# Eight edits around TensorE's row of matmuls in a two-layer transformer trunk on one Trainium2 core

## What is computed

```python
def nsa_compress(kv, pos, w1, b1, w2, b2):       # 15 overlapping blocks of 32 tokens
    ...
    hid = jax.nn.gelu(flat @ w1 + b1)
    return hid @ w2 + b2

def nsa_attention(q, k_cmp, v_cmp, k_slc, v_slc, k_win, v_win, gates):
    ...                                           # 8 heads of 64 in 2 groups, queries in blocks of 128
        s_c = jnp.einsum('bgrqd,bgnd->bgrqn', qq, kc)
        p_c = masked_softmax(s_c, cmp_end[None, :] <= tq[:, None])
        o_c = jnp.einsum('bgrqn,bgnd->bgrqd', p_c.astype(vc.dtype), vc)
    ...
    y = gates[..., 0:1] * to_bthd(o_c) + gates[..., 1:2] * to_bthd(o_s) + gates[..., 2:3] * to_bthd(o_w)

def token_mixer(x, w_in, ...):
    hcat = x @ w_in
    ...                                           # y_a: attention, y_b: short convolution, y_c: retention
    proj = jnp.einsum('btcw,cwd->btcd', ys, w_br)
    gates = jax.nn.sigmoid(mgate).reshape(b, t, N_BRANCHES, D_MODEL)
    return jnp.sum(gates * proj, axis=2) @ w_out

def moe_swiglu(x, w_router, w_gate, w_up, w_down):
    logits = (x @ w_router).astype(jnp.float32)
    top_v, top_i = lax.top_k(logits, TOP_K)
    probs = jax.nn.softmax(top_v, axis=-1)
    ...
        out = out + combine[..., e:e + 1] * swiglu(x, w_gate[e], w_up[e], w_down[e])

def reference(x, w_in, ...):
    for l in range(DEPTH):
        m = token_mixer(x, ...)
        x = layer_norm(ALPHA * x + m, ln1_g[l], ln1_b[l])
        if l % 2 == 0:
            f = swiglu(x, ...)
        else:
            f = moe_swiglu(x, ...)
        x = layer_norm(ALPHA * x + f, ln2_g[l], ln2_b[l])
    return x
```

## Time and profile before

| | |
|---|---|
| runs, us | 1846.99, 1847.23, 1847.29 (median 1847.23) |
| profiled execution, own time, us | 1848.0 |
| its span, us | 1846.1 |
| TensorE busy, matmul / weight load | 99% / 86% |
| VectorE, ScalarE, GpSimd busy | 79%, 64%, 3% |
| instructions | 29565 |
| DMA over the span | 511 MB, mean 277 GB/s |
| granted clock, mean | 0.996 |

### The profile page before, as it was taken

How to read it: one execution, slowest core, us unless ns; L and a number is a source line. 1 busy time by engine, 2 the same in 40 slices (tenths; PEclk the granted TensorE clock), 3 DMA queues, 4 the chain that set the end, 5 groups by cost and what they waited for, 6 DMA issues and landing times.

```text
span 1846.1 us, 29565 instructions
## 1 busy us (share of the span) xinstructions
PE 1820.9 (99%) x10905; PEld 1587.3 (86%) x10905; DVE 1457.5 (79%) x1670; ACT 1179.3 (64%) x1441; POOL 56.1 (3%) x37
## 2 busy tenths in 40 slices
PE   9999999999999999999999999999999999999996
PEld 8999998999979999997888888888888888888884
DVE  6675677544566675668999989999999999999998
ACT  6544444443447444446778787787787877877874
POOL 0000000000000000002101001000010010100100
PEclk9999999999999999999999999999999999999998
DMA  9544445555537333455999999999999999999994
GB/s 379 190 162 147 169 165 184 183 196 188 182 137 270 141 138 138 160 206 192 378 375 353 379 362 376 378 337 390 370 354 381 357 376 375 334 395 369 357 381 171
DMA packets 72478, 511.07 MB, mean 277 GB/s; under 512 B 8160, under 2 KB 8544, under 8 KB 11616
## 3 DMA queue, kind: packets, MB, share of 16 engines
q1 hardware_dynamic: 69552, 498.09, 71.4%
q0 software_dynamic: 1584, 5.77, 1.0%
q10 hardware_dynamic: 1280, 6.32, 0.9%
HBM read 508.06 MB, written 2.10 MB: 276 GB/s over the span
## 4 chain that ended last, share of the span: by engine, by line
PE 87%; DVE 6%; ACT 3%; issue 2%; DMA 1%; SPq 0%; DVEq 0%; ACTq 0%
PE PS L398 16%; PE PS L400 16%; PE PS L399 16%; PE PS L371 10%; PE PS L372 10%; PE PS L373 10%; DVE w_lo L1273 2%; DVE w_lo L1270 1%; PE PS L825 1%; DVE merged L1762 1%; ACT w_hi L913 1%; PE PS L557 1%; PE PS L589 1%; PE PS L384 1%; DMA raw<-wstream 1%
## 5 line engine op out<-in xcount | busy, mean ns | idle before, releaser
L1270 DVE TENSOR_TENSOR w_lo<-raw,w_hi 128x1024 fp32r<-128x1024 f32 x471 | 575.3, 1221 | 223.1 <-ACT w_hi L913 221.8
L913 ACT ACTIVATE w_hi<-raw 128x1024 fp32r<-128x1024 f32 x471 | 499.1, 1060 | 274.7 <-PE PS L400 203.6
L1273 DVE TENSOR_TENSOR w_lo<-raw,w_hi 128x1024 fp32r<-128x1024 f32 x471 | 573.4, 1217 | 0.0
L914 ACT ACTIVATE w_hi<-raw 128x1024 fp32r<-128x1024 f32 x471 | 493.5, 1048 | 0.0
L398 PE MATMUL PS<-w_hi,xT_hi 128*128 128x512 f32 x960 | 380.0, 396 | 0.6 <-DVE w_lo L1273 0.2
L371 PE MATMUL PS<-xT_hi,w_hi 128*128 128x256 f32 x1312 | 376.3, 287 | 0.2 <-DVE w_lo L1273 0.2
L400 PE MATMUL PS<-w_hi,xT_lo 128*128 128x512 f32 x960 | 374.5, 390 | 0.0
L399 PE MATMUL PS<-w_lo,xT_hi 128*128 128x512 f32 x960 | 373.8, 389 | 0.0
L372 PE MATMUL PS<-xT_lo,w_hi 128*128 128x256 f32 x1312 | 371.1, 283 | 0.0
L373 PE MATMUL PS<-xT_hi,w_lo 128*128 128x256 f32 x1312 | 371.0, 283 | 0.0
L371 PEld LDWEIGHTS PS<-xT_hi,w_hi 128*128 128x128 f32 x1312 | 251.3, 192 | 9.1 <-issue 6.8
(11 more groups left out here) (261 smaller groups left out, 1567.5 us busy)
## 6 DMA issues: line engine op xcount, KB each, us to landing
raw<-wstream SPq DMA_DIRECT2D x471, 1024.0 KB, 6.8
soft<-ln ACTq DMA_DIRECT2D x4, 1024.0 KB, 5.6
X<-x SPq DMA_DIRECT2D x2, 512.0 KB, 4.1
raw<-wstream SPq DMA_DIRECT2D x4, 256.0 KB, 7.2
x_rows<-X ACTq DMA_DIRECT2D x1, 1024.0 KB, 4.9
out<-X ACTq DMA_DIRECT2D x2, 512.0 KB, 3.7
cst<-consts SPq DMA_DIRECT2D x1, 906.0 KB, 14.5
sm<-small SPq DMA_DIRECT2D x1, 364.5 KB, 15.7
```

The lines of the kernel that those rows point to most:

```text
L913: activate(w_hi[:, at % RING, 0:SUB // 2], src[:, 0:SUB // 2], ACT.Copy).then_inc(half_done, 1)
L914: activate(w_hi[:, at % RING, SUB // 2:SUB], src[:, SUB // 2:SUB], ACT.Copy).then_inc(hi_done, 1)
L1270: v.tensor_tensor(w_lo[:, at % RING, 0:SUB // 2], src[:, 0:SUB // 2], w_hi[:, at % RING, 0:SUB // 2], ALU.subtract)
L1273: v.tensor_tensor(w_lo[:, at % RING, SUB // 2:SUB], src[:, SUB // 2:SUB], w_hi[:, at % RING, SUB // 2:SUB], ALU.subtract).then_inc(lo_done, 1)
```

## The change

- A "cmp" step turns four heads at a time. Probabilities are stored with a pitch of 32 columns per head (`cprobs`), two transposes of 128 x 128 put four heads below one another, and ScalarE alone copies the 256 columns. For this, `Vc` holds for each of four heads V in rows 32n to 32n+14 and zeros else, and the product with it is made per head over 128 rows: four matmuls of 128 columns in place of two of 256. `compressed_kv` makes V for 128 output rows from `hidV`, the hidden values repeated four times at a pitch of 32 (ScalarE writes them so), and VectorE copies four 15-row pieces in place of one. The zeros come from three memsets at the start.
- In the norm after the dense block, tile 0 is taken up in halves like tile 1, on a new semaphore `first_ps`.
- `first_unit` waits for halves of `xT_hi` and `xT_lo` of the second token tile where it needs them.
- The router's fillers go from 7 and 4 to 4 and 3.
- The first subtile is loaded in two transfers; VectorE makes all four quarters of its remainder between the third and the fourth block of `xT_lo`.
- At an item's start, the first two pieces of `add_scattered` stand ahead of the split of subtile 5.
- At the end, statistics of both tiles come ahead of both tiles' scaling, and tile 0's stand between the third and the fourth addition. The store of tile 1 goes in two halves.
- GpSimd's last gather takes 16 rows in place of 128.

```diff
             for t in range(TT):
                 sp.dma_start(X[:, t, :], x[t * P:(t + 1) * P, :]).then_inc(x_in[t], 16)
-            for c in range(4):
-                at = slice(c * SUB // 4, (c + 1) * SUB // 4)
-                sp.dma_start(raw[:, 0, at], wstream[0][:, at]).then_inc(landed[0] if c == 3 else part_in[c], 16)
+            for c in range(2):
+                at = slice(c * SUB // 2, (c + 1) * SUB // 2)
+                sp.dma_start(raw[:, 0, at], wstream[0][:, at]).then_inc(landed[0] if c else part_in, 16)
...
             def first_unit(n, bank, slot, ready=None):
-                pe.wait_ge(xT_hi_rdy, 2 * TT * (n + 1))
+                def high_ready(k):
+                    if k % 4 == 0:
+                        pe.wait_ge(xT_hi_rdy, 2 * TT * n + 3 + k // 4)
+                    if ready:
+                        ready(k)
+
+                def low_ready(k):
+                    if k % 4 == 0:
+                        pe.wait_ge(xT_rdy, 2 * TT * n + 3 + k // 4)
...
                 pe.wait_ge(xT_rdy, 2 * TT * n + 1)
-                o = fm_first(bank, slot, 0, ready)
-                pe.wait_ge(xT_rdy, 2 * TT * (n + 1))
-                fm_first_low(o, slot, 0)
-                return fm_first_low(fm_first(bank, slot, 1), slot, 1)
+                o = fm_first(bank, slot, 0, high_ready)
+                fm_first_low(o, slot, 0, low_ready)
+                return fm_first_low(fm_first(bank, slot, 1, both_ready), slot, 1, both_ready)
...
-                        last = tm_block([o for o in outs if o[1] == t], (s + n) % RING, lhs, ks[n], cols,
-                                        cols == 512 and n == 0, n == 1)
+                        own = [o for o in outs if o[1] == t]
+                        if t == 0 and n == 1 and b is not None:
+                            tm_block(own[:1], (s + n) % RING, lhs, ks[n], cols, False, True).then_inc(first_ps, 1)
+                            own = own[1:]
+                        last = tm_block(own, (s + n) % RING, lhs, ks[n], cols, cols == 512 and n == 0, n == 1)
...
-                        o = PS[0:NC, MB, 64 + g * DH:64 + (g + 1) * DH]
+                        o = PS[:, MB, 64 + g * DH:64 + (g + 1) * DH]
                         for c in range(2):
-                            mm(o, hidT[:, 2 + c, g * NC:(g + 1) * NC], sm[:, l, S_W2V + c * DH:S_W2V + (c + 1) * DH],
+                            mm(o, hidV[:, c, g].rearrange("p a n -> p (a n)"), sm[:, l, S_W2V + c * DH:S_W2V + (c + 1) * DH],
...
                     if kind == "cmp":
-                        for n in range(NH):
-                            last = mm(PS[0:NC, TB + n // 4, (n % 4) * P:(n % 4 + 1) * P], cprob[:, n, :], ident,
-                                      start=True, stop=True)
+                        for par in range(2):
+                            last = nc.tensor.transpose(PS[:, TB, par * P:(par + 1) * P], cprobs[:, 4 * par:4 * par + 4]
+                                                       .rearrange("p i n -> p (i n)"), ident)
...
                     if a == 1:
-                        for par in range(2):
-                            last = mm(o[par], Vc[:, g, :],
-                                      cprobT[0:NC, (4 * par + 2 * g) * P:(4 * par + 2 * g + 2) * P], start=False,
-                                      stop=True, skip_group_check=True)
+                        for e in range(2):
+                            for par in range(2):
+                                last = mm(o[par][:, e * P:(e + 1) * P], Vc[:, 2 * g + e, :],
+                                          cprobT[:, par * P:(par + 1) * P], start=False, stop=True,
+                                          skip_group_check=True)
...
-                stay_busy(7)
+                stay_busy(4)
                 pe.wait_ge(cnt_in, 1)
...
-                stay_busy(4)
+                stay_busy(3)
...
             norm(4)
-            for t in range(TT):
-                act.wait_ge(norm_rdy, 2 * TT * 3 + 2 * t + 2)
-                act.dma_start(out[t * P:(t + 1) * P, :], X[:, t, :]).then_inc(out_dma, 16)
-            act.wait_ge(out_dma, 16 * TT)
+            act.wait_ge(norm_rdy, 2 * TT * 3 + 2)
+            act.dma_start(out[0:P, :], X[:, 0, :]).then_inc(out_dma, 16)
+            act.wait_ge(norm_rdy, 2 * TT * 3 + 3)
+            act.dma_start(out[P:T, 0:512], X[:, 1, 0:512]).then_inc(out_dma, 16)
+            act.wait_ge(norm_rdy, 2 * TT * 3 + 4)
+            act.dma_start(out[P:T, 512:D], X[:, 1, 512:D]).then_inc(out_dma, 16)
+            act.wait_ge(out_dma, 16 * 3)
...
-                nc.gpsimd.indirect_dma_start(xg, None, x_rows, bass.IndirectOffsetOnAxis(ap=rows[:, 0:1], axis=0),
+                few = P if i < NI - 1 else 16
+                nc.gpsimd.indirect_dma_start(xg[0:few], None, x_rows,
+                                             bass.IndirectOffsetOnAxis(ap=rows[0:few, 0:1], axis=0),
...
                 if n < 4:
+                    if n == 2:
+                        dve.wait_ge(half_ps if t else first_ps, 1)
+                        chain.link(add_x(n, t, 0))
+                        stats(n, t, 0)
+                        halves = (1,)
...
-                        if n == 0 and b >= 2:
-                            first_part(b - 2)
+                        if n == 0 and b == 2:
+                            for c in range(4):
+                                first_part(c)
...
+                    add_scattered(i, (0, 1))
                     split(MOE0 + 5, i * NB)
-                    add_scattered(i, (0, 1))
...
-                add_scattered(n_items, range(4))
+                add_scattered(n_items, (0, 1, 2))
+                dve.wait_ge(acc_rdy, n_items * 4 + 4)
+                for c in range(2):
+                    last = stats(4, 0, c)
+                add_scattered(n_items, (3,))
+                chain.link(last)
+                aggregate(0)
...
```

90 lines of the change are left out of this document (53 added, 37 removed).

## The result

The changed kernel takes 1836.38 us (median of 5 runs, 1835.74 to 1838.7), the one before 1847.21 (5 runs, 1846.23 to 1847.29). The ratio is 0.9948, 95% interval 0.9937 to 0.9959: 9.6 us less, between 7.6 and 11.6 (the two medians are 10.8 apart). The forecast was 1835.9, the range 1832.8 to 1839.3.

What follows compares the result with a forecast made beforehand. TensorE, busy for 99% of the span with instructions in a row, was taken to bound the kernel. The terms summed to -11.3 us off the median of 1847.23, giving 1835.9 us, range 1832.8 to 1839.3.

Steps and rivals of the forecast that it cites:

- Compressed transposes: Four compressed attention steps: two padded transposes replace eight identity products (16 instructions), saving 1.73 us each; -7.2 us, bounds -7.3 and -6.3.
- rival (e): Compressed attention steps: each padded transpose is two instructions, so the time is 1836.8 us; chance 0.03.
- V of the compression: Compression's V half: 128 output rows rather than 15 make its twelve instructions slower; +0.6 us over two layers, bounds +0.3 to +1.3.
- Products with V: Eight places, four matmuls of 128 columns for two of 256: extra slot time against a vanished pause; 0, bounds -1.1 and +1.3.
- First units: After two norms, TensorE starts without the last quarter of the high parts; -0.35 us in all, bounds -0.5 and 0.
- Front: First subtile in two transfers, not four; TensorE's 1.3 us of waits bound the gain; +0.1 us, bounds -0.5 and +0.8.
- Router: Fewer fillers let the counting matmuls start nearer VectorE's choice, 1.0 us being lost there; -0.95 us, bounds -1.3 and 0.
- Rival (b): Router: fewer fillers leave TensorE idle between count and picks, its clock returns later, losing 1.3 or 2.6 us; chance 0.10.
- Rival (d): Clock stays at its lower level far into the first expert item; for 35 us the time would be 1853; chance 0.02.
- Expert items: Two accumulations ahead of subtile 5's split use up its 1.39 us slack; +0.1 us, bounds 0 and +1.0 over eight items.
- End: Earlier last write, smaller last store and 16-row last gather end the run at 1843.1; -3.0 us, bounds -1.2 and -3.6.
- Rival (a): GpSimd ends last, a small indirect gather costing as much as a large one; end saves 1.2, time 1837.7; chance 0.12.

## Why the prediction was right, and where it was not

**What bounds the kernel** was right: TensorE's row of instructions. Its busy time fell by 6.2 us (5 to 8 forecast), and behind the front the places ahead of the router add up to the same gain in every trace.

**Compressed transposes**: -7.31 against -7.2, at the edge of the bounds: the up to 0.1 us of dead time at the entry, named and only in part taken, came whole at each step (0.21 to 0.12 us). Real transposes of 128 x 128 with padding cost as those of the full step do, one instruction each, so rival (e) falls.

**V of the compression**: +0.71 per layer, where +0.3 was taken. The step that failed is the choice between +0.25 "if the pauses between its groups vanish" and "+0.6 if they stay". They stay, and grow with the output rows, from 0.15 to 0.20 us, with 0.16 for the instruction behind; only the one ahead of them shrinks, by 0.09. The bounds for both layers, +0.3 to +1.3, just miss the 1.42.

**Products with V**: -0.14 to -0.15 each, where 0 was taken, from the bounds -1.1 to +2.3. Both effects were named, a slot more and a pause less. The slot term was mis-sized: +0.16 was taken, from starts within 0.44 us, and four pairs of 128 columns have theirs within 0.33, so it is +0.06. The pause ahead of the group went as foreseen (0.10); a second one of 0.10, behind it, was not in the sum.

**Norm**: -0.73 against -0.57, inside the bounds. **First units**: -0.66 against -0.35 and outside the bounds: a whole slot of 0.22 us had been kept for the last filler, and the first unit starts 0.03 us behind it.

**Front**: -0.69 against +0.1, outside the bounds. The step that failed is "TensorE loses only 1.3 us in all to its parts", "which bounds the gain", and what followed from it: the look was at the first subtile alone. The gain is at the second, whose transfer stands behind the first one's issues on SyncE's queue: in SyncE's timeline its issue moved from 4.00 to 3.04 us.

**Router**: +0.97 in the profiled pair against -0.95. The wrong step is "1.0 us lost". One execution was read, in which the clock's lower level happened to lie on the fillers; at the upper level the fillers are done 1.5 us after their start and VectorE's choice is ready 1.8 us after it (838.47 to 840.29 in the trace with seven and four), so nothing is there to be saved. Rival (b) had the mechanism and its price, 1.3 or 2.6 us; the profiled run paid 1.9 more than was forecast. It got a chance of 0.10, because "the fillers end when the data come", which is true of seven and not of four: it looked for idle time between the count and the picks, and the 0.85 us lie ahead of the count. Rival (d), a clock that stays down far into the experts, did not show in any of the nine traces with four fillers.

**Expert items**: +0.75 against +0.1, inside the bounds, but not by the mechanism they were made for.

**End**: -1.87 in the pair, -2.2 as a mean over the seven traces that have the changed end (14.7 to 15.4), against -3.0; against the mean of the three traces with the old end (17.67) it would be -2.6. The store's part was right or better: VectorE's last write moved by 1.07 us (0.7 forecast), the last piece took 2.1 us here and in two others of the seven traces and 2.8 to 2.9 in the rest (2.0 to 2.6 forecast), and with the gather out of the way the end is at -4.1. Rival (a) was half right: GpSimd ends last, but not because a small gather costs as much as a large one (3.0 to 3.8 us for 16 rows, 3.9 to 6.2 for the gathers of 128 rows at the end of all traces). What the sum missed is that the three gathers wait for one another: the first two took 4.5 and 4.6 us where they had 4.25 and 4.33, so the last was issued 10.45 us after TensorE's last matmul in place of 9.82. And 1.74 us of closing lie behind its landing, where a store has 0.4 to 0.8; the prediction had up to 2.0 for this among its bounds and took an end 1.1 us too early.

**The time**, then, was met because misses of both signs cancelled, which is luck: the front, the transposes, the products with V, the norm and the first units gave 2.5 us more than forecast, and V of the compression, the items, the end and the router took 4.5 more in the profiled run, less where the clock's lower level was shorter. The prediction's outer bounds are also not the sum of its terms' bounds, as it says: these add up to 1832.5 and 1844.8, not 1831 and 1843.

**The signs** that it named came on both sides. Of those for "right", the transposes, the busy time, the norm and the last store came; the count does follow VectorE's choice, but the clock was not back before the gather, and GpSimd's last gather landed 0.9 us behind the store. Of those for "wrong", a span that ends on GpSimd came, and the low clock lasted to 846.4, some 855 in the kernel before by the matmul stream. The fifth subtile of an item took 0.15 us longer, with no wait that the profile lists, and the next one made up for it.

## What to carry to other kernels

Where an engine stands in an unbroken row of instructions, the gain of fewer instructions is read to hundredths from places in the same trace that already use the cheaper form. A place where the clock was down is read from more than one execution before fillers are taken out, and they are timed against the engine that they wait for at full clock. Where a queue issues transfers one behind the other, a transfer saved is worth most to what is queued behind it; and at the end of a kernel each queue's last transfer is followed with what its engine needs to close.

## What the runs showed of the hardware

- The clock's lower level came at the router in stretches of 3.4 or 6.8 us, or not at all, in executions of almost the same program; the router stretch went from 16.4 to 18.8 us with it.
- An indirect gather on GpSimd took 3.0 to 3.8 us for 16 rows of 4 KB beside two stores of 256 KB, 4.0 beside a store of 512 KB, and 5.3 for 128 rows beside the two stores. Where the span ended on GpSimd, it ended 1.73 or 1.74 us behind that landing.
- Four pairs of fp32 matmuls with 128 rows, 64 columns and 128 moving columns have their starts 0.10 us apart, pair by pair.
- An expert item took 121.20 us in both kernels without the compressed edits and 121.28 to 121.30 in all with them, though its instructions are the same. The cause is open.
